# Mixer of a two-layer block: differential scores as three single-speed passes, sparse branch's side work and weight halves in other steps, another order where stages meet

## The chip, the cores and the metric

The kernel runs on one core of a Trainium2 chip. TensorE (PE) does the matrix products and transposes, VectorE (DVE) and ScalarE (ACT) the elementwise work and the copies out of PSUM, GpSimd (POOL) very little here, and SyncE (SP) issues most DMAs. Every engine has its own instruction stream and waits on semaphores of the others. The metric is the device time of one execution in microseconds; the times below are medians of runs of the same program.

## The reference, cut to what matters

```python
def second_block(x, ...):                      # after first_block, a hybrid layer
    for l in range(DEPTH_2):                   # 2 layers; x is 512 x 1024, fp32
        ...
        h = _rmsnorm(x, norm_g[l, 0]) * (1.0 + sc0) + sh0
        x = x + 0.5 * g0 * _swiglu(h, ffn_w_gate[l, 0], ffn_w_up[l, 0], ffn_w_down[l, 0])
        h = _rmsnorm(x, norm_g[l, 1]) * (1.0 + sc1) + sh1
        x = x + g1 * _token_mix(h, w_in[l], w_out[l], ...)
        h = _rmsnorm(x, norm_g[l, 2]) * (1.0 + sc2) + sh2
        x = x + 0.5 * g2 * _swiglu(h, ffn_w_gate[l, 1], ffn_w_up[l, 1], ffn_w_down[l, 1])
    return _rmsnorm(x, final_g)

def _token_mix(h, w_in, w_out, ...):
    z = h @ w_in
    (gu, gv, dq, dk, dv, nq, ...) = jnp.split(z, pts, axis=-1)
    y_a = _gmlp_sgu(gu, gv, ...)               # spatial gating, 4 groups of 64
    y_b = _diff_attention(dq, dk, dv, ...)     # "differential branch", 4 heads x 2 maps of 32
    y_c = _nsa(nq, ...)                        # "sparse branch", 8 heads of 64
    return jnp.concatenate([y_a, y_b, y_c], axis=-1) @ w_out

# in _diff_attention, for a block of 128 queries
        s = jnp.einsum('bhmqd,bhmkd->bhmqk', qi, k).astype(jnp.float32) * scale
        p = _masked_softmax(s, t[:, None] >= pos[None, :])
        a = p[:, :, 0] - lam * p[:, :, 1]
```

## The kernel before

The instruction streams of all engines are written out by hand; there is no scheduler. Each branch of a stage is a generator with numbered steps, one generator for each engine, and the stage's functions call next() on them between pieces of dense work. An engine runs its stream strictly in order, so what a step waits for holds back all that is written behind it.

**Dense products.** Activations and weights are kept as sums of two fp32r tensors, a high and a low one, and `three` (L545 to 548) forms each product with three matmuls: low activation by high weight (L546), high by high (L547), high by low (L548). fp32r is the form that TensorE streams in one pass; plain fp32 operands take two passes of it, which the trace records as two matmuls. A unit of weights, 128 partitions by 2048 columns, arrives as `raw`; ACT copies it into `w_hi` (L508) and DVE subtracts into `w_lo` (L514), in halves of 1024 columns. act_w and dve_w stand for these, and their last argument chooses a half.

**The order of stages.** After the first block come two layers, each of a gated feed-forward stage, the mixer and a second feed-forward stage. In the mixer, pe_mixer (L2782), act_mixer (L2895) and dve_mixer (L2987) run the differential branch (pe_da L2168, 22 steps) and the sparse branch (pe_nsa L2523, act_nsa L2736, dve_nsa L2654, 36 steps) between the dense products: input projections for the first part, and then the rows of the output projection, units o1_0, o1_1, o2_0, o2_1. PE is given one step of a branch after every few dense triples.

**Differential scores.** Queries and keys after rotation are `dq` and `dk`, fp32, four pieces of 128x512 (p = 0, 1 for dq, 2, 3 for dk), the last operation of each being an addition on DVE (L2159). In each of steps 0 to 15, PE multiplies one block of 128 queries by (b+1)*128 keys for two maps m (L2179). The contraction is only 32 long: the two maps use different groups of 32 rows of the array and different PSUM banks. Widths 512, 128, 384 and 256 take turns, four of each in a layer.

**Sparse branch.** Step s computes the scores of item s on PE (L2542) into two PSUM banks (N_SC). These banks come free when DVE has run `smallest` (L2664) on them, which finds the row minimum; ACT then takes the exponential, DVE runs `norm` (L2673, L2678), PE transposes, DVE or ACT copies back (L2646, L2644), and PE multiplies by the values (L2569). In dve_nsa the order inside a step is: smallest(s), copy, norm(s-1), and then the "side chains": the compressed-key scores (cm L2476, cx L2479 and L2481, cn), the gating branch's statistics g1, g3 (L2722, L2724), g5, gm, g7, g8, and the splits of finished pieces of the activation into high and low.

**Weight halves in the mixer.** Those of the output projection are prepared between steps. Before the change, ACT does the halves of o1_0 after steps 12 and 17, and DVE after 13 and 19; o1_1 follows on ACT after 20 and 22, o2_0 after 26 and 28. PE begins o1_0 two steps after item 16 and takes next(nsa) after every second activation row.

**Where the mixer meets the next stage.** pe_tail ends the mixer with unit o2_1; the second feed-forward stage begins in pe_first (L1903) with the units g and u, each for the first half of the sequence (H0, 256 columns) and then the second (H1). act_to_h (L1923) and dve_to_h (L1948) form its input from the residual update `xup` (L794), the statistics of the norm, and the modulation, which gives `h_hi` (L736) and `h_lo` (L745), one of eight pieces at a time.

## Time and profile before

| | us |
|---|---|
| median of the runs | 2634.02 (2633.14 to 2635.98, 3 runs) |
| profiled execution, its own time | 2635.69 |
| its span | 2634.3 |
| mean granted TensorE clock | 0.997 |

The span is the time from the first to the last instruction of the profiled execution; the 1.4 us around it belong to the launch. A timeline has one row for each instruction, or for a run of equal ones (x4), with its start in microseconds from the beginning of the span, its duration, and in square brackets the time that the engine idled before it and what released it. Matmuls are pipelined: a row's duration reaches past the start of the next one, so what a matmul costs is the distance from its start to the next start. The letter m below is a map, "step" is a numbered step of one of the branches, and "layer 1" lies 1011.1 us behind layer 0 with the same waits, so that one layer is enough to read.

### The profile page before, as it was taken

What the parts mean: (1) busy time and instruction counts of PE and PEld (TensorE: products, weight loads), DVE (VectorE), ACT (ScalarE), POOL (GpSimd) and SP (SyncE); (2) the same over time, 40 slices, a digit from 0 to 9 for tenths busy, and PEclk for the clock granted to TensorE, in tenths of its full rate; (3) what the DMA queues carried; (4) which work ended last, traced back from release to release, by engine and by line L of the source; (5) the groups of instructions that cost most, each with busy time, mean ns of one, the idle gap of its engine ahead of it and who ended that gap; (6) DMA issues with size and microseconds to landing.
All of it is one profiled execution on the core that took longest, in us unless ns stands there. A gap on an engine that the chain in (4) does not pass through costs nothing.

```text
span 2634.3 us, 33757 instructions
## 1 busy us (share of the span) xinstructions
PE 2602.2 (99%) x13925; PEld 2150.1 (82%) x13925; DVE 1558.8 (59%) x2769; ACT 1036.7 (39%) x1795; POOL 15.0 (1%) x43
## 2 busy tenths in 40 slices
PE   8999999999999999999999999999999999999999
PEld 5788888898888897767888889888888776888888
DVE  7766554458666366777766637653346687633334
ACT  4652343444222245665322225222234665422223
POOL 1000000000000000000000000000000000000000
PEclk9999999999999999999999999999999999999999
DMA  8255433225555234312655424532233501222222
GB/s 261 80 176 172 130 119 112 80 81 193 206 186 182 89 111 116 112 33 68 213 199 191 161 84 156 206 130 96 96 96 107 149 27 49 95 98 96 96 92 68
DMA packets 298241, 330.13 MB, mean 125 GB/s; under 512 B 13411, under 2 KB 248679, under 8 KB 298089
## 3 DMA queue, kind: packets, MB, share of 16 engines
q1 hardware_dynamic: 297716, 327.44, 38.2%
q8 instruction: 110, 1.80, 0.3%
q10 hardware_dynamic: 372, 0.55, 0.1%
q14 instruction: 43, 0.34, 0.0%
HBM read 319.56 MB, written 2.10 MB: 122 GB/s over the span
## 4 chain that ended last, share of the span: by engine, by line
PE 95%; DVE 4%; ACT 1%; DMA 0%; SPq 0%; issue 0%; DVEq 0%
PE bank L546 27%; PE bank L548 27%; PE bank L547 27%; PE bank L600 2%; PE bank L2542 2%; PE bank L2569 1%; PE bank L2179 1%; PE bank L574 1%; PE bank L575 1%; PE bank L576 1%; DMA mw<-in_w_mod 0%; PE bank L2354 0%; PE bank L903 0%; DVE w_lo L514 0%; DVE E L2678 0%; PE bank L590 0%
## 5 line engine op out<-in xcount | busy, mean ns | idle before, releaser
L546 PE MATMUL bank<-h_lo,w_hi 128*128 128x512 f32 (+1 forms) x2496 | 935.7, 375 | 2.3 <-DVE h_lo L745 1.2
L548 PE MATMUL bank<-h_hi,w_lo 128*128 128x512 f32 (+1 forms) x2496 | 918.5, 368 | 0.0
L547 PE MATMUL bank<-h_hi,w_hi 128*128 128x512 f32 (+1 forms) x2496 | 917.3, 368 | 0.0
L514 DVE TENSOR_TENSOR w_lo<-raw,w_hi 128x1024 fp32r<-128x1024 f32 (+1 forms) x420 | 489.1, 1200 | 373.5 <-ACT w_hi L508 373.3
L508 ACT ACTIVATE w_hi<-raw 128x1024 fp32r<-128x1024 f32 (+1 forms) x420 | 420.1, 1036 | 349.7 <-PE bank L548 335.4
L546 PEld LDWEIGHTS bank<-h_lo,w_hi 128*128 128x128 f32 x2496 | 471.0, 189 | 85.8 <-issue 4.9
L547 PEld LDWEIGHTS bank<-h_hi,w_hi 128*128 128x128 f32 x2496 | 471.4, 189 | 78.5 <-issue 3.9
L548 PEld LDWEIGHTS bank<-h_hi,w_lo 128*128 128x128 f32 x2496 | 470.3, 188 | 78.5
L546 PE MATMUL bank<-a_lo,w_hi 128*128 128x512 f32 (+1 forms) x1056 | 388.2, 368 | 4.4 <-DVE w_lo L514 4.4
L548 PE MATMUL bank<-a_hi,w_lo 128*128 128x512 f32 (+1 forms) x1056 | 384.8, 364 | 0.0
L547 PE MATMUL bank<-a_hi,w_hi 128*128 128x512 f32 (+1 forms) x1056 | 384.3, 364 | 0.0
L546 PEld LDWEIGHTS bank<-a_lo,w_hi 128*128 128x128 f32 x1056 | 199.5, 189 | 35.7 <-DVE w_lo L514 4.9
L548 PEld LDWEIGHTS bank<-a_hi,w_lo 128*128 128x128 f32 x1056 | 199.4, 189 | 31.4
L547 PEld LDWEIGHTS bank<-a_hi,w_hi 128*128 128x128 f32 x1056 | 199.6, 189 | 30.6
L767 ACT ACTIVATE a_hi<-tmp 128x512 fp32r<-128x512 f32 x104 | 65.5, 632 | 388.7 <-DVE tmp L2075 370.1
L794 DVE SCALAR_TENSOR_TENSOR x<-bank,small,x 128x512 f32<-128x512 f32 (+1 forms) x152 | 99.2, 663 | 182.0 <-PE bank L548 181.7
L2024 ACT ACTIVATE tmp<-bank 128x512 f32<-128x512 f32 x88 | 52.1, 596 | 292.8 <-PE bank L548 292.8
L2075 DVE TENSOR_TENSOR tmp<-tmp,bank 128x512 f32<-128x512 f32 x88 | 60.2, 684 | 124.8 <-PE bank L548 124.8
L771 DVE TENSOR_TENSOR a_lo<-tmp,a_hi 128x512 fp32r<-128x512 f32 x104 | 71.9, 692 | 68.6 <-ACT a_hi L767 68.4
L652 DVE SCALAR_TENSOR_TENSOR nacc<-swf,small,nacc 128x512 f32<-128x512 f32 x105 | 78.8, 751 | 3.2
L652 DVE SCALAR_TENSOR_TENSOR tmp<-swf,small,tmp 128x512 f32<-128x512 f32 x105 | 78.8, 751 | 3.2
L600 PEld LDWEIGHTS bank<-res,E 128*128 128x128 f32 x428 | 47.4, 142 | 27.0 <-issue 17.3
(347 smaller groups left out, 2283.7 us busy)
## 6 DMA issues: line engine op xcount, KB each, us to landing
swf<-in_w_ada SPq DMA_DIRECT2D x60, 1024.0 KB, 7.5
raw<-in_ffn_w_gate SPq DMA_DIRECT2D x44, 1024.0 KB, 5.2
raw<-in_ffn_w_up SPq DMA_DIRECT2D x44, 1024.0 KB, 5.2
raw<-in_w_in SPq DMA_DIRECT2D x40, 1024.0 KB, 5.0
raw<-in_ffn_w_down SPq DMA_DIRECT2D x32, 1024.0 KB, 5.3
raw<-in_w_in SPq DMA_DIRECT2D x32, 512.0 KB, 5.2
raw<-in_ffn_w_down SPq DMA_DIRECT2D x16, 768.0 KB, 4.4
mw<-in_w_mod SPq DMA_DIRECT2D x8, 1024.0 KB, 12.0
```

The source lines that it names most:

```text
L508: nc.scalar.activation(o, r, ACT.Copy).then_inc(*w_hi.up((i, h)))
L514: nc.vector.tensor_tensor(o, r, half(w_his[place_of[i]], i, h)[0].bitcast(F32), ALU.subtract).then_inc(*w_lo.up((i, h)))
L546: nc.tensor.matmul(o, w1, al, start=start, stop=False)
L547: nc.tensor.matmul(o, w1, ah, start=False, stop=False)
L548: return nc.tensor.matmul(o, w2, ah, start=False, stop=stop)
L600: return nc.tensor.transpose(o, i, ident[0:n, 0:n])
L652: nc.vector.scalar_tensor_tensor(acc, v[:, a, :], cv[:, k:k + 1], acc, ALU.mult, ALU.add).then_inc(*dve.up(("acc", st, j, k)))
L767: nc.scalar.activation(a_hi[:, c, :], src, ACT.Copy).then_inc(*act.up(("ah",) + key))
L771: nc.vector.tensor_tensor(a_lo[:, c, :], src, a_hi[:, c, :].bitcast(F32), ALU.subtract).then_inc(*dve.up(("a",) + key))
L794: nc.vector.scalar_tensor_tensor(x[:, c, COLS[hv]], ps.of(key)[:, COLS[hv]], gain[:, c:c + 1], x[:, c, COLS[hv]], ALU.mult, ALU.add).then_ ...
L2075: nc.vector.tensor_tensor(t, t, ps.of(("u", st, f))[:, :], ALU.mult).then_inc(*dve.up(("mul", st, f), lets=("u", st, f)))
L2542: nc.tensor.matmul(t[par][:, 0:w], nq[r, c * 512 + b * 128:c * 512 + b * 128 + 128], (ks, kw)[br][r, k0:k0 + w], start=True, stop=True).th ...
```

## The change

It has five parts.

1. **Differential scores.** The rotated queries and keys become high and low fp32r pairs, d_hi and d_lo. For each of the four pieces ACT makes a copy (act_da_high) and DVE a subtraction (dve_da_low). The scores of a step are then six fp32r matmuls in place of two fp32 ones (which the trace records as four): for each of low by high, high by low, high by high, both maps.
2. **Side chains of the sparse branch** are spread over more steps: cm in step 1 and cx in step 2 (before both in step 1), cn in step 4, g1 in step 9 and g3 in step 10 (before both in 9), gm in 12 at the latest, the second g7, g8 and split one to two steps later, the last subtraction of a finished output piece (OC_LOW) one step later, the transposes around steps 5 to 8 one step later.
3. **Weight halves in other steps.** o1_0: ACT after steps 12 and 14, DVE after 13 and 16. o1_1: ACT as before, DVE after 20 and 21 in its own count of pairs of steps, as shown in the diff. o2_0: ACT after 24 and 26, DVE correspondingly one pair earlier, and the first half of o2_1 before the end of the branch.
4. **Output rows between the last steps.** The dense work of o2_0 is written out, and steps 33, 34 and 35 of the sparse branch stand between its triples, not all ahead of it.
5. **Meeting order** after a mixer. The first half of u's weights is split in the tail, the norm's sums are taken from within g (at piece 4) to within u (at piece 3), u's banks are taken only when u begins, and the residual updates of the second half of the sequence stand after the modulation of the first, apart from one of them.

Cut to its core (name changes and the further shifts by one step are left out):

```diff
@@ sb tensors
-    dq = sb("dq", 1024, at=at_a + 16384 + 4096)
-    dk = sb("dk", 1024, at=at_a + 8192)
+    d_hi = [sb("dq_hi", 1024, F32R, at=at_a + 16384 + 4096), sb("dk_hi", 1024, F32R, at=at_a + 8192)]
+    d_lo = [sb(n, 1024, F32R, at=phase0 + 56256 + 4096 * i) for i, n in enumerate(("dq_lo", "dk_lo"))]
@@ act_tail, and the same with dve_w in dve_tail
+        if st[0] == "m":
+            act_w(first_of(nxt)[1], 0, 0)
@@ pe_first
-                    elif before(st) is not None and name == us[0][0] and j == 4:
+                    elif before(st) is not None and (name, j) == ((us[1][0], 3) if late else (us[0][0], 4)):
                         pe_sums(st, 1)
@@ act_to_h
+        if b4[0] == "m":
+            second = {3: [lambda: act_w(first[1], 0)], 6: second[1], 7: second[3] + second[5]}
+        else:
+            second[2] = [lambda: act_w(first[1], 0, 0)]
+            second[4] = [lambda: act_w(first[1], 0)]
@@ dve_to_h
+        elif b4[0] == "m":
+            second = dve_second(st, b4, gain)
+            dve_modulate(st, 0, mu, add, {5: second[0] + second[1]})
+            dve_w(first_of(st)[1], 0)
+            for i in range(2, 6):
+                second[i][0]()
@@ new
+    def act_da_high(l, p):
+        act.wait_ge(dve, ("rx", l, p))
+        nc.scalar.activation(da_part(d_hi, p), pair(p)[1][:, :], ACT.Copy).then_inc(*act.up(("rh", l, p)))
+
+    def dve_da_low(l, p):
+        dve.wait_ge(act, ("rh", l, p))
+        nc.vector.tensor_tensor(da_part(d_lo, p), pair(p)[1][:, :], da_part(d_hi, p).bitcast(F32), ALU.subtract).then_inc(
+            *dve.up(("rd", l, p)))
@@ pe_da
-                for m in range(2):
-                    t = bank(("ds", l, s, m), M_SC)
-                    pe.wait_ge(dve, ("rd", l, 3))
-                    r = slice((par * 2 + m) * 32, (par * 2 + m) * 32 + 32)
-                    nc.tensor.matmul(t[:, 0:w], dq[r, c * 512 + b * 128:c * 512 + b * 128 + 128],
-                                     dk[r, c * 512:c * 512 + w], start=True, stop=True).then_inc(*pe.up(("ds", l, s, m)))
+                for i, (dq, dk) in enumerate(((d_lo[0], d_hi[1]), (d_hi[0], d_lo[1]), (d_hi[0], d_hi[1]))):
+                    for m, r in enumerate(rows):
+                        mm = nc.tensor.matmul(t[m][:, 0:w], dq[r, q], dk[r, k], start=i == 0, stop=i == 2)
@@ dve_cm, dve_nsa
             if s == 1:
                 dve_cm(l, 1)
+            if s == 2:
+                dve_cx(l, 1)
@@ dve_nsa
             if s == 9:
                 dve.wait_ge(act, ("gl", l, 1))
                 nc.vector.tensor_reduce(m16, v3, AX, ALU.add).then_inc(*dve.up(("g1", l)))
-                dve.wait_ge(dve, PREV)
+            if s == 10:
+                dve.wait_ge(dve, ("g1", l))
                 nc.vector.scalar_tensor_tensor(v3, mb, -1.0 / 64, v3, ALU.mult, ALU.add).then_inc(*dve.up(("g3", l)))
@@ act_mixer
-                if m and s == 0:
-                    act_w(("gu", l), 1, 0)
+                if m and s in (0, 2):
+                    act_w(("gu", l), 1, s // 2)
...
-            if s == 17:
-                act_w(("gu", l))
             if s in (20, 22):
                 act_w(("o1", l, 0), 1, s // 22)
-            if s in (26, 28):
-                act_w(("o1", l, 1), 1, s // 28)
+            if s in (24, 26):
+                act_w(("o1", l, 1), 1, s // 26)
+            if s == 28:
+                act_w(("o2", l, 0), 1, 0)
@@ dve_mixer
         for c in range(NK):
-            for _ in range(2):
-                next(nsa)
-            if c == 1:
+            next(nsa)
+            if c == 0:
                 dve_w(("gu", l))
+            next(nsa)
             if c in (2, 3):
                 dve_w(("o1", l, 0), 1, c - 2)
-            if c in (5, 6):
-                dve_w(("o1", l, 1), 1, c - 5)
+            if c in (4, 5):
+                dve_w(("o1", l, 1), 1, c - 4)
+            if c == 6:
+                dve_w(("o2", l, 0), 1, 0)
@@ pe_mixer
-        for _ in nsa:
-            pass
+        next(nsa)
         u = unit(("o2", l, 0))
+        for j, k in enumerate(O2_ROWS):
+            pe.wait_ge(dve, ("a", ("m", l), k))
+            for c in range(4):
...
+                m = three(fills[c][:, :], w1, w2, a_lo[:, k, :], a_hi[:, k, :], j == 0, j == 3)
...
+                if (j, c) in ((0, 1), (1, 0), (1, 3)):
+                    next(nsa)
```

(The name in act_w and dve_w is the unit that runs while the next one is prepared: act_w(("gu", l), 1, 0) makes the first half of o1_0, act_w(("o1", l, 0), 1, ...) those of o1_1, act_w(("o1", l, 1), 1, ...) those of o2_0.)

How the change moves the instructions is seen at three places. The first is DVE in steps 1 and 2 of the sparse branch. `gmb<-gmb,hsum` ends step 1's small work, E_6_172 is the compressed-key score tile (cm, cx), E_4_170 and E_5_171 are the score tiles that `smallest` reads. Before:

```order
L2380 TENSOR_TENSOR gmb<-gmb,hsum 64x256
L2476 TENSOR_TENSOR E_6_172<-bank,res 128x512
L2479 TENSOR_REDUCE small<-E_6_172 128x16
L2481 TENSOR_TENSOR E_6_172<-E_6_172,small 128x512
L2664 ISA E_4_170,small<-bank,res 128x128
L2664 ISA small 128x1
L2664 ISA E_5_171,small<-bank,res 128x128
```

With the change:

```order
L2413 TENSOR_TENSOR gmb<-gmb,hsum 64x256
L2508 TENSOR_TENSOR E_6_172<-bank,res 128x512
L2699 ISA E_4_170,small<-bank,res 128x128
L2699 ISA small 128x1
L2699 ISA E_5_171,small<-bank,res 128x128
L2699 ISA small 128x1
L2708 RECIPROCAL small<-small 128x2
L2713 TENSOR_SCALAR E_2_168<-E_2_168,small,gates 128x512
L2713 TENSOR_SCALAR E_3_169<-E_3_169,small,gates 128x512
L2514 TENSOR_REDUCE small<-E_6_172 128x16
L2516 TENSOR_TENSOR E_6_172<-E_6_172,small 128x512
```

The reduction and the subtraction now stand behind the next step's `smallest` and norm instead of ahead of them.

The second place is DVE around the second low half of o1_0 (w_lo_59). Before, it stands behind step 19:

```order
L2646 COPY tmp_64<-bank 128x512
L2673 RECIPROCAL small<-small 128x2
L2678 TENSOR_SCALAR E_4_170<-E_4_170,small,gates 128x128
L2678 TENSOR_SCALAR E_5_171<-E_5_171,small,gates 128x128
L514 TENSOR_TENSOR w_lo_59<-raw_54,w_hi_57 128x1024
L794 SCALAR_TENSOR_TENSOR x<-bank,small,x 128x512
L2664 ISA E_0_166,small<-bank,res 128x384
```

With the change it stands behind step 16:

```order
L2681 COPY tmp_173<-bank 128x384
L2708 RECIPROCAL small<-small 128x2
L2713 TENSOR_SCALAR ex_179<-ex_179,small,gates 128x256
L2713 TENSOR_SCALAR ex_180<-ex_180,small,gates 128x256
L514 TENSOR_TENSOR w_lo_59<-raw_54,w_hi_57 128x1024
L2699 ISA E_2_168,small<-bank,res 128x512
L2699 ISA small 128x1
```

It moved up by three steps of the branch and one residual update.

The third place is PE at the end of the sparse branch, between the last transposes (L600) and the last products with the values (L2569 before, L2604 after; `vsw`). Before:

```order
L600 MATMUL bank<-res,ex_179 128x128 x2
L600 MATMUL bank<-res,ex_180 128x128 x2
L2569 MATMUL bank<-ps_175,vsw 64x128
L2569 MATMUL bank<-ps_176,vsw 64x128
L2569 MATMUL bank<-ps_175,vsw 64x128
L2569 MATMUL bank<-ps_176,vsw 64x128
```

With the change:

```order
L600 MATMUL bank<-res,ex_179 128x128 x2
L600 MATMUL bank<-res,ex_180 128x128 x2
L546 MATMUL bank<-a_lo,w_hi_57 128x512
L547 MATMUL bank<-a_hi,w_hi_57 128x512
L548 MATMUL bank<-a_hi,w_lo_59 128x512
L546 MATMUL bank<-a_lo,w_hi_57 128x512
L547 MATMUL bank<-a_hi,w_hi_57 128x512
L548 MATMUL bank<-a_hi,w_lo_59 128x512
L546 MATMUL bank<-a_lo,w_hi_57 128x512
L547 MATMUL bank<-a_hi,w_hi_57 128x512
L548 MATMUL bank<-a_hi,w_lo_59 128x512
L2604 MATMUL bank<-ps_175,vsw 64x128
```

Three triples of o2_0 now stand between the transposes and the products that use what is copied back from them.

## Rows read from the trace of the kernel before

**Rows 1.** Page, part 1: busy time of each engine and share of the span.

```profile
PE 2602.2 (99%) x13925; PEld 2150.1 (82%) x13925; DVE 1558.8 (59%) x2769; ACT 1036.7 (39%) x1795; POOL 15.0 (1%) x43
```

**Rows 2.** Waits of PE: released line, releaser, total us, times, longest.

```profile
PE bank L546 <- DVE w_lo L514: 5.4, 4, 2.2
...
PE bank L2542 <- DVE small L2664: 1.4, 4, 0.5
PE bank L546 <- DVE h_lo L745: 1.2, 4, 0.3
PE bank L2604 <- DVE gvv L2730: 0.7, 2, 0.4
...
PE bank L600 <- DVE ps L2646: 0.6, 2, 0.3
```

**Rows 3.** Timeline of PE: fp32 products on 32 rows, two full-array ones.

```profile
1016.43 1.13 PE L2179 MATMUL bank<-dk,dq 32*128 32x512 f32 x4
1017.49 0.50 PE L546 MATMUL bank<-h_lo,w_hi 128*128 128x512 f32 x1
...
1024.43 0.49 PE L2179 MATMUL bank<-dk,dq 32*128 32x128 f32 x4
1024.85 0.50 PE L546 MATMUL bank<-h_lo,w_hi 128*128 128x512 f32 x1
...
72.40 1.02 PE L1112 MATMUL bank<-uc,wrg 128*128 128x512 f32 x2
73.26 1.02 PE L1114 MATMUL bank<-uc,wig 128*128 128x512 f32 x2
```

**Rows 4.** Timeline of PE: starts of dense fp32r triples of 512 and 256 columns.

```profile
1236.11 0.39 PE L546 MATMUL bank<-a_lo,w_hi 128*128 128x512 f32 x1
...
1236.79 0.28 PE L546 MATMUL bank<-a_lo,w_hi 128*128 128x256 f32 x1
...
1237.15 0.28 PE L546 MATMUL bank<-a_lo,w_hi 128*128 128x256 f32 x1
```

**Rows 5.** Timeline of DVE: the last addition of the rotated keys.

```profile
1010.76 0.69 DVE L2159 TENSOR_TENSOR dk<-swap,tmp 128x512 f32<-128x512 f32 x1
```

**Rows 6.** Timeline, DVE and then PE: sparse steps 1 to 3.

```profile
1105.49 0.68 DVE L2476 TENSOR_TENSOR E<-bank,res 128x512 f32<-128x512 f32 x1
...
1106.92 0.69 DVE L2481 TENSOR_TENSOR E<-E,small 128x512 f32<-128x512 f32 x1
1107.53 0.28 DVE L2664 CUSTOM_DVE_ANT_0 E<-bank,res 128x128 f32<-128x128 f32 x1
...
1108.18 0.49 PE L2542 MATMUL bank<-kw,nq 64*128 64x128 f32 x4 [1.32 <-DVE small L2673]
```

**Rows 7.** DVE, PE; windows: length; busy PE, PEld, DVE, ACT, POOL, clock, DMA share, GB/s.

```profile
1173.25 1.22 DVE L514 TENSOR_TENSOR w_lo<-raw,w_hi 128x1024 fp32r<-128x1024 f32 x1
...
1174.53 0.50 PE L546 MATMUL bank<-a_lo,w_hi 128*128 128x512 f32 x1 [2.19 <-DVE w_lo L514]
...
1175.80:1179.20 3.40, 3.40 (x12) 1.73 (x11) 1.11 (x5) 0.00 (x0) 0.00 (x0) 0.50 0.88 298
1174.53:1184.95 10.42, 10.42 (x64) 6.50 (x65) 4.66 (x14) 4.52 (x11) 0.00 (x0) 0.84 0.32 102
1204.89:1213.72 8.83, 8.83 (x67) 5.73 (x66) 6.88 (x19) 5.12 (x12) 0.00 (x0) 1.00 0.00 0
```

**Rows 8.** Timeline, PE and then DVE: the meeting after the mixer of layer 0.

```profile
1251.63 0.39 PE L546 MATMUL bank<-h_lo,w_hi 128*128 128x256 f32 x1 [0.15 <-DVE h_lo L745]
1252.95 0.39 PE L546 MATMUL bank<-h_lo,w_hi 128*128 128x256 f32 x1 [0.35 <-DVE h_lo L745]
1257.86 0.39 PE L546 MATMUL bank<-h_lo,w_hi 128*128 128x256 f32 x1 [0.52 <-DVE w_lo L514]
...
1259.65 0.48 DVE L745 SCALAR_TENSOR_TENSOR h_lo<-tmp,small,h_hi 128x256 fp32r<-128x256 f32 x1
...
1260.44 0.48 DVE L745 SCALAR_TENSOR_TENSOR h_lo<-tmp,small,h_hi 128x256 fp32r<-128x256 f32 x1
```

More of the change, by code:

```diff
@@ L335, in carve, with here @@
         place = [start]
-        def here(name, cols):
-            t = sb(name, cols, at=place[0])
+        def here(name, cols, dt=F32):
+            t = sb(name, cols, dt, at=place[0])
             place[0] += (cols * 4 + 63) // 64 * 64
@@ L1903, in pe_first @@
     def pe_first(st, units_, ring):
-        us = [(name, unit(name), [(key, bank(key, ring)) for key in keys]) for name, keys in units_]
+        us, fills_of = [(name, unit(name), keys) for name, keys in units_], {}
+        late = before(st) is not None and before(st)[0] == "m"
+        if not late:
+            fills_of = {name: [(key, bank(key, ring)) for key in keys] for name, _, keys in us}
         for hv in range(2):
-            for name, u, fills in us:
+            for name, u, keys in us:
                 def hook(j):
@@ L1916, in hook @@
                         pe_norm(st, 1)
-                    elif before(st) is not None and name == us[0][0] and j == 4:
+                    elif before(st) is not None and (name, j) == ((us[1][0], 3) if late else (us[0][0], 4)):
                         pe_sums(st, 1)
+                if name not in fills_of:
+                    fills_of[name] = [(key, bank(key, ring)) for key in keys]
+                fills = fills_of[name]
                 dense(name, fills if hv else [(None, t) for _, t in fills], u, 0, H, NK,
@@ L2123, in rope_where @@
         every = slice(0, 128)
-        if p < 2:
-            d = [(every, dq[:, p * 512:p * 512 + 512])]
-        elif p < 4:
-            d = [(every, dk[:, (p - 2) * 512:(p - 2) * 512 + 512])]
+        if p < 4:
+            d = [(every, pair(p)[1][:, :])]
         elif p < 8:
@@ L2737, in act_nsa @@
         for s in range(36):
+            m16 = stl[0][:, 0:16]
             if s % 2 == 0:
                 nsa_copy(act, l, s - 3)
+            if s == 12:
+                act.wait_ge(dve, ("g5", l))
+                nc.scalar.activation(m16, m16, use(ACT.Ln), scale=1.0 / 64, bias=eps_c).then_inc(*act.up(("gn", l)))
+                act.wait_ge(act, PREV)
+                nc.scalar.activation(m16, m16, use(ACT.Exp), scale=-0.5).then_inc(*act.up(("g6", l)))
             if s < 32:
@@ L2910, in act_mixer @@
         act_w(("dv", l))
-        for tb in range(4):
-            act_dv(l, tb)
+        act_dv(l, 0)
+        act_dv(l, 1)
+        act_da_high(l, 2)
+        act_dv(l, 2)
+        act_da_high(l, 3)
+        act_dv(l, 3)
         da = act_da(l)
@@ L3010, in dve_mixer @@
         dve_rope(l, 1)
+        dve_da_low(l, 0)
+        dve_da_low(l, 1)
         dve_w(("dv", l))
```

91 lines of the change are left out of this document (53 added, 38 removed).

## The prediction

> **What bounds the kernel now.** I read the busy times first. PE is busy for 2602.2 of 2634.3 us [rows 1], so whatever is gained must come out of the few microseconds in which PE waits, or out of the matmuls themselves. DVE (59%) and ACT (39%) have room on average, and only their order can hurt. The second view is the list of what PE waits for [rows 2]. Nearly all of it in the mixer is DVE's: the low half of a weight (5.4 us in 4 waits), the release of score banks, the gating branch's `gvv`. The third is PE's timeline around each of these waits, and there DVE's rows just ahead of it. The waits come in pairs, one for each layer, so I cost one layer and double it.
>
> **Scores of the differential branch.** Before, a step of width 512 takes 1017.49 - 1016.43 = 1.06 us from its start to the next operation's, and one of width 128 takes 1024.85 - 1024.43 = 0.42 [rows 3]. The line through both is 0.20 + 0.00167 us for each column, which puts widths 256 and 384 at 0.63 and 0.85. Does the pair of maps run side by side or one after the other? One full-array fp32 product of 512 columns, in its two passes (x2), takes 73.26 - 72.40 = 0.86 us [rows 3]. Two maps in 1.06 us are 0.20 + 0.86, so the pair costs one product: they run together on their different rows. The 0.20 does not grow with the width.
>
> After, a step is three passes of such a pair. A dense fp32r pass takes (1236.79 - 1236.11) / 3 = 0.227 us for 512 columns and (1237.15 - 1236.79) / 3 = 0.12 for 256 [rows 4], so about 0.173 for 384. For 128 no such pass is in these rows: 0.06 is the floor (half of 256), 0.12 the ceiling. I take 0.12, since changing the stationary operand costs the same however few columns stream. That makes 0.20 + 0.68 = 0.88, 0.72, 0.56 and 0.56 us, against 1.06, 0.85, 0.63 and 0.42: -0.18, -0.13, -0.07 and +0.14, together -0.24 us. Each width comes four times a layer: **-1.0 us**. With the floor for width 128 it would be -1.7.
>
> Are the loads of the later passes hidden? The second pass of today's step has no load of its own in the sum: width 128 comes out at 0.42 with 0.20 fixed, which leaves 0.11 for each pass and nothing beside it [rows 3]. The Trainium skill speaks against that for the new passes ("TensorE: Matmul & The Clock Gate", Part 3, The mechanism): a weight load overlaps a running matmul only if the two use different row groups, and here each pass reloads the rows of the pass before. By the rows the sum for the scores is -1.0 a layer, by the rule it would be +1.4; the rows of today's two passes don't agree with the rule, so it is rival 2 with a small chance.
>
> The pairs' preparation adds four ACT copies and four DVE subtractions of 128x512 a layer, some 0.7 us each by the addition of the same size [rows 5]. The last rotated key is written at 1010.76 + 0.69 = 1011.45, the first score starts at 1016.43 [rows 3, 5]. 5.0 us cover the last subtraction and what ACT puts in front of it (some 2.7 us by the same price), so I cost it at nothing. If the cover were gone, each further us would be one on the path.
>
> **Side chains.** The scores of sparse step 3 wait 1.32 us for score banks [rows 6]. DVE runs the two operations of cx (the second ends at 1107.53, the first began after cm's start at 1105.49) ahead of `smallest`, which begins at 1107.53. Without cx it begins after cm alone, 0.7 us after 1105.49, so 1.3 us earlier, and the wait is gone: **-1.3**. What is late next is `smallest` of step 3, behind the displaced cx. From step 3 to step 4 PE has 0.42 of scores, 1.44 of four triples of 256 columns [rows 4] and, as an estimate, 1.0 of transposes, 2.9 in all; DVE has `smallest` 0.4, norm 1.1, cx 1.3, 2.8 in all. It is on the edge, and I leave 0 to 0.3 us for it in the range. The same mechanism stands behind one of the two L2542 waits in a layer that are released by `smallest` (L2664: 1.4 us in 4, [rows 2]; the longest, 0.5, is behind g1 and g3, which the change puts into two steps): **-0.5**; the other one, 0.2 at step 1, stays. The `gvv` wait, 0.4, goes with gm a step earlier: **-0.4**.
>
> **Weight halves.** At 1174.53 o1_0's third block had waited 2.19 us for a low half that DVE began at 1173.25, 1.22 us long [rows 7]. The subtraction now stands three steps and one residual update earlier. A step is some 4 us of PE's time, and the wait is about 2.2, so it goes with room: **-2.2**. What follows that wait counts as well: from 1175.80 to 1179.20 the granted clock is 0.50, that is 1.2 GHz in place of 2.4, and PE had just stood still for 2.19 us. The stretch 1174.53 to 1184.95 holds 64 matmuls in 10.42 us, the like stretch 1204.89 to 1213.72 67 in 8.83 at clock 1.00 [rows 7]: 1.6 us. I expect the clock to stay up if PE does not stop: **-1.6**. Against it stands that the DMA share in those 3.4 us is 0.88, so that something other than the idle time could be the cause; that is a rival.
>
> **Output rows between the last steps.** The wait of 0.3 for the last copy back (L2646 to `ps`) [rows 2] is covered by three triples, 2.0 us at 0.68 [rows 4]: **-0.3**. These steps' banks come free later by that much, which nobody needs.
>
> **Meeting.** Before, PE waits 0.15, 0.35 and 0.52 us here [rows 8]. The third, for u's low weights, goes, because half of them is split in the tail. DVE makes one piece of `h_lo` every 1260.44 - 1259.65 = 0.79 us [rows 8], and PE uses it up in two triples of 256 columns, 0.72 us [rows 4], so small waits stay. The second half's pieces now come behind four residual updates and one low half of 1.22 us that follow the modulation, about when PE is there. I take 0.4 of the 1.0 us as left: **-0.6**, with bounds -1.0 (all three gone) and +0.5 (the second half late by one low half, 1.2, less what the third gives).
>
> **Exposed loads.** A matmul after a wait has its weight load in the open: 0.50 us against 0.39 for the same operation [rows 4, 7], 0.1. Five waits go: **-0.5**.
>
> **The sum** for a layer is -1.0 - 1.3 - 0.5 - 0.4 - 2.2 - 1.6 - 0.3 - 0.6 - 0.5 = -8.4 us, for both -16.8. The profiled execution was 2635.69 us with a span of 2634.3; it would be 2618.9 with 2617.5. It lies 1.7 above the median of 2634.02, so against the median the forecast is **2617.2 us**, with a range of its own of 2613 to 2621.5 (narrow passes at their floor -1.4, the meeting -0.8 or +2.2, the displaced cx +0.6, 1.5 for unseen shifts).
>
> **The rivals.**
> 1. *The clock drops all the same, and waits return.* Everything on DVE moves earlier, but DVE's work in the mixer is not less, it has four subtractions more. If the half clock belongs to the DMA burst, +3.2; if `smallest` waits return at half their size behind cx and the splits, +1.8 to +3. Together some +6.3: 2623.5 us. For it: the DMA share in the half-clock stretch. Against it: no other wait of the mixer's is followed by such a stretch.
> 2. *The load of each pass in the open.* The second and third pass of the three wider widths take 0.1 more each: 24 steps by 0.2, +4.8; a pass of 128 columns has its load in the 0.12 already: 2622.0 us. Against it is the width-128 step above. This is what the skill's rule would give.
> 3. *The pairs don't run together in fp32r.* The rows show pairs only for plain fp32. Six passes in a row are 0.20 + 6 x 0.227 = 1.56, 1.24, 0.92, 0.92 us: +0.50, +0.39, +0.29, +0.50, that is +1.7 for four widths, +13.4 in place of -1.9 for the kernel: 2632.5 us, no change that could be measured.
> 4. *The same, and a load in the open at every change of rows*: five more of 0.1 us in 32 steps, +16: 2648.5 us, **slower**. It decides from where a step costs more than about 0.5 us above the present one, on the average of the widths (0.5 x 32 = 16, which eats up the other gains). For it: a change between full-array and 32-row work costs 0.20 today. Against it: the pair of today starts together.
> 5. *The weight half does not come earlier.* The order permits it, but its raw weights may arrive late: the 2.2 and 1.6 us of both layers stay, 2617.2 + 7.6 = 2624.8 us. Against it: the first half of the same unit is already being used when PE waits.
>
> **How the numbers follow.** Forecast 0.60, rival 1 0.18, rival 2 0.08, rival 3 0.04, rival 4 0.05, rival 5 0.05. A measurement of this kernel can tell 0.2%, 5.3 us, from no change. Below 2628.7 lie the forecast and rivals 1, 2 and 5, 0.91, of which I take off 0.04 for waits that I have not seen: faster 0.87, within 0.2% 0.08, slower 0.05. From 2612 to 2627 lie the forecast's own range but for a tenth, rivals 1, 2 and 5 and most of what is between them: about 0.8.
>
> **What would show it.** In the profile after: a score step of the differential branch of 0.88 us at width 512 and 0.56 at 128 (1.56: rival 3; 1.06 and 0.7: rival 2); no L546 wait for `w_lo` above 0.3 us and a clock of 1.00 where o1_0's third block runs; no L2542 wait above 0.3 in sparse step 3 and step 10; waits of some 0.4 in all at the meeting. The prediction is wrong if PE's list of waits has a new entry of a microsecond or more in the mixer, or if PE's busy time rises.

## The result and the profile after

| | before | changed | ratio, 95% interval |
|---|---|---|---|
| median of the runs, us | 2633.58 (2631.75 to 2635.98, 4 runs) | 2620.74 (2619.85 to 2622.49, 4 runs) | 0.9947 (0.9936 to 0.9959) |
| profiled execution, us | 2635.69 | 2622.49 | |
| its span, us | 2634.3 | 2621.2 | |

The change makes the kernel 14.0 us faster by the ratio (10.8 to 16.9). The forecast was a gain of 16.8 us and a time of 2617.2 us, with a range of 2612 to 2627. The busy times and the list of PE's waits answer to [rows 1] and [rows 2]:

```profile
PE 2593.9 (99%) x13989; PEld 2153.6 (82%) x13989; DVE 1562.8 (60%) x2777; ACT 1041.1 (40%) x1803; POOL 15.0 (1%) x43
```

```profile
PE bank L2577 <- DVE small L2699: 2.9, 6, 0.6
...
PE bank L2211 <- DVE small L2296: 1.3, 2, 0.6
PE bank L709 <- DVE nacc L703: 1.0, 2, 0.5
```

L2577 is the line of the sparse scores (L2542 before), L2211 that of the differential ones (L2179), L2699 `smallest` (L2664), L2681 the copy back (L2646). The 5.4 us of waits for `w_lo` are gone, and so are the 1.3 us at step 3 and `gvv`. What is waited for score banks of the sparse branch behind `smallest` has grown: six waits of 2.9 us where four made 1.4 (plus 2.6 behind the norm). Two entries are new, 1.3 us for score banks of the differential branch (L2211) and 1.0 us for the norm's sums (nacc). The prediction had said that a new entry of a microsecond or more in the mixer would show it wrong; this sign came, although the time is inside the range. PE's busy time, its other sign, fell from 2602.2 to 2593.9 us. Of the 1.3 us at L2211 little is a loss: before, a pause of 0.53 us stood inside the same step, between its two maps, where no wait is listed.

Both kernels issue the same dense matmuls in the same order, so the start of the n-th one can be compared between the two traces. I call these the dense starts. Their differences, taken across one place after another, divide the gain. Layer 1, in us:

| place | forecast (with its load, 0.1 each) | measured |
|---|---|---|
| differential scores, 16 steps | -1.0 | -1.15 |
| banks at sparse step 3 | -1.4 | -1.37 |
| banks behind g1, g3 | -0.6 | -0.60 |
| `gvv` | -0.5 | -0.43 |
| low half of o1_0 | -2.3 | -2.47 |
| half clock behind it | -1.6 | -1.56 |
| banks at sparse step 23 | 0 | +0.60 |
| last steps of the sparse branch, the banks at step 31 included | -0.4 | -0.33 |
| norm's first sums | 0 | +0.78 |
| rest of the meeting | -0.6 | -1.04 |
| sum | -8.4 | -7.57 |

Layer 0 gives -7.64. Both give -15.2; the spans differ by only 13.1, since the changed kernel's profiled execution had lost 2.06 us before the first mixer, in code that the change doesn't touch: 0.4 at the start and 1.67 at 612 to 620 us, where the granted clock stayed low for longer (below).

The score steps, answering to [rows 3]:

```profile
1018.49 0.49 PE L2211 MATMUL bank<-dk_hi,dq_lo 32*128 32x512 f32 x2
1018.82 0.40 PE L2211 MATMUL bank<-dk_lo,dq_hi 32*128 32x512 f32 x2
1019.05 0.40 PE L2211 MATMUL bank<-dk_hi,dq_hi 32*128 32x512 f32 x2
1019.38 0.50 PE L546 MATMUL bank<-h_lo,w_hi 128*128 128x512 f32 x1
...
1026.16 0.33 PE L2211 MATMUL bank<-dk_hi,dq_lo 32*128 32x128 f32 x2
1026.32 0.27 PE L2211 MATMUL bank<-dk_lo,dq_hi 32*128 32x128 f32 x2
1026.43 0.27 PE L2211 MATMUL bank<-dk_hi,dq_hi 32*128 32x128 f32 x2
1026.63 0.50 PE L546 MATMUL bank<-h_lo,w_hi 128*128 128x512 f32 x1
```

Width 512 takes 1019.38 - 1018.49 = 0.89 us (1.06 before, 0.88 forecast), width 128 takes 0.48 (0.42 before, 0.56 forecast). The two maps of a pass start together (x2). The third pass follows the second at 0.23 and 0.11 us, with no load in the open, while the second follows the first at 0.33 and 0.16. At widths 384 and 256 the steps take 0.72 and 0.55.

DVE at sparse steps 1 and 2, answering to [rows 6]:

```profile
1106.42 0.68 DVE L2508 TENSOR_TENSOR E<-bank,res 128x512 f32<-128x512 f32 x1
1107.02 0.27 DVE L2699 CUSTOM_DVE_ANT_0 E<-bank,res 128x128 f32<-128x128 f32 x1
...
1108.54 0.68 DVE L2514 TENSOR_REDUCE small<-E 128x16 f32<-128x512 f32 x1
1109.26 0.69 DVE L2516 TENSOR_TENSOR E<-E,small 128x512 f32<-128x512 f32 x1
```

`smallest` now starts 0.6 us after cm began; before, 2.04 us after it. PE has no wait there.

The stretch from the start of o1_0's third block, answering to the windows of [rows 7] (columns as there):

```profile
1170.59:1180.20 9.61, 9.61 (x70) 6.39 (x69) 7.00 (x22) 5.92 (x14) 0.00 (x0) 1.00 0.00 0
```

The clock is 1.00 all through, and there is no wait. At the meeting none of the three waits of [rows 8] is in the list any more. But over the second half of the sequence PE now runs at DVE's pace, every second triple 0.79 us behind the last one where it was 0.72 before:

```profile
1258.83 0.36 PE L546 MATMUL bank<-h_lo,w_hi 128*128 128x256 f32 x1
...
1259.62 0.36 PE L546 MATMUL bank<-h_lo,w_hi 128*128 128x256 f32 x1
```

One place did not go as forecast: PE waits for score banks at sparse step 23, which the `smallest` of step 22 releases. The rows show this wait, and then what DVE does meanwhile:

```profile
1184.10 0.70 PE L2577 MATMUL bank<-kw,nq 64*128 64x256 f32 x4 [0.63 <-DVE small L2699]
...
1180.79 0.68 DVE L2752 TENSOR_TENSOR a_lo<-bank,a_hi 128x512 fp32r<-128x512 f32 x1
1181.39 1.22 DVE L514 TENSOR_TENSOR w_lo<-raw,w_hi 128x1024 fp32r<-128x1024 f32 x1
1182.52 0.75 DVE L794 SCALAR_TENSOR_TENSOR x<-bank,small,x 128x512 f32<-128x512 f32 x1
1183.18 0.41 DVE L2699 CUSTOM_DVE_ANT_0 E<-bank,res 128x256 f32<-128x256 f32 x1
```

Three operations, 2.4 us, stand in DVE's queue ahead of `smallest`: the subtraction of a finished output piece, moved there by OC_LOW, a weight half and a residual update. The last two stood there before the change as well, and the subtraction one step earlier, where DVE had been idle:

```profile
1181.98 0.69 DVE L2715 TENSOR_TENSOR a_lo<-bank,a_hi 128x512 fp32r<-128x512 f32 x1 [1.44 <-ACT a_hi L2766]
...
1186.31 1.22 DVE L514 TENSOR_TENSOR w_lo<-raw,w_hi 128x1024 fp32r<-128x1024 f32 x1
1187.45 0.74 DVE L794 SCALAR_TENSOR_TENSOR x<-bank,small,x 128x512 f32<-128x512 f32 x1
1188.11 0.41 DVE L2664 CUSTOM_DVE_ANT_0 E<-bank,res 128x256 f32<-128x256 f32 x1
```

So this half of o1_1 is not one of those that the change moved on DVE; the diff has its line unchanged. The same three kinds of operation meet again eight steps later, where PE waits 0.63 us at step 31. And at the norm's sums:

```profile
1239.33 0.70 PE L709 MATMUL bank<-nacc,res 128*128 128x256 f32 x2 [0.52 <-DVE nacc L703]
...
1222.69 0.43 DVE L2681 COPY ps<-bank 128x256 f32<-128x256 f32 x1 [2.09 <-PE bank L600]
1226.64 0.69 DVE L2752 TENSOR_TENSOR a_lo<-bank,a_hi 128x512 fp32r<-128x512 f32 x1 [3.52 <-ACT a_hi L2811]
1227.59 3.50 DVE L514 TENSOR_TENSOR w_lo<-raw,w_hi 128x1024 fp32r<-128x1024 f32 x3 [0.26 <-ACT w_hi L508]
```

DVE stands idle for 2.09 and 3.52 us, and then has three low halves in a row, behind which the updates and the sums are late.

### The profile page after: what moved, and what is told of

Its sections match the earlier page's. It is cut to its first block, busy times and chain, and to the rows that moved or that the text cites. A ratio compares the mean times of both kernels' runs of the same rounds, so it can differ in the third digit from the quotient of the medians.

```text
span 2621.2 us, 33927 instructions
## 1 busy us (share of the span) xinstructions
PE 2593.9 (99%) x13989; PEld 2153.6 (82%) x13989; DVE 1562.8 (60%) x2777; ACT 1041.1 (40%) x1803; POOL 15.0 (1%) x43
## 4 chain that ended last, share of the span: by engine, by line
PE 95%; DVE 3%; ACT 1%; DMA 0%; SPq 0%; issue 0%; DVEq 0%
PE bank L546 27%; PE bank L548 27%; PE bank L547 27%; PE bank L600 3%; PE bank L2577 2%; PE bank L2604 2%; PE bank L2211 1%; PE bank L574 1%; PE bank L575 1%; PE bank L576 1%; DVE w_lo L514 1%; DMA mw<-in_w_mod 0%; PE bank L907 0%; PE bank L2387 0%; DVE x L794 0%; PE bank L590 0%
## 5 line engine op out<-in xcount | busy, mean ns | idle before, releaser
L600 PE MATMUL bank<-res,E 128*128 128x128 f32 x428 | 67.8, 283 | 0.6 <-DVE tmp L2681 0.6
```

What stands on the lines that cost most here:

```text
L600: return nc.tensor.transpose(o, i, ident[0:n, 0:n])
```

## Experiments

**One part alone: the scores (e1_split).** The kernel before with the preparation and the scores of the change, as in the diff ahead.

> The kernel before with one part of the change: the differential scores as three fp32r passes of a pair of maps, with their four copies and four subtractions a layer. Theory: the new passes run in pairs and their weight loads are hidden, whatever stands around them. A step should take 0.89, 0.72, 0.55 and 0.48 us at widths 512, 384, 256 and 128, as in the profile of the changed kernel, instead of 1.06, 0.85, 0.63 and 0.42: -0.31 for each set of four widths, eight sets, -2.5 us in all, about 2631.1. Rival: the preparation (eight operations more on ACT and DVE) delays what follows, so that part of it is lost, and the time stays within 1 us of before.

Median 2633.44 us against 2635.42 in the same session, ratio 0.9993 (0.9984 to 1.0003): a gain of 1.8 us that is not clear of noise. The dense starts show it more sharply: -1.11 us across the differential branch in layer 0 and -1.13 in layer 1, with no loss behind it, 2.2 us in all. The rest of the expected 2.5 went to PE's wait for score banks in the last step (0.65 us; before it was 0.53 and stood between the two maps of that step).

**One part alone: the weight half (e2_half).** The kernel before with

```diff
-                if m and s == 0:
-                    act_w(("gu", l), 1, 0)
+                if m and s in (0, 2):
+                    act_w(("gu", l), 1, s // 2)
...
-            if s == 17:
-                act_w(("gu", l))
...
-            for _ in range(2):
-                next(nsa)
-            if c == 1:
+            next(nsa)
+            if c == 0:
                 dve_w(("gu", l))
+            next(nsa)
```

> The kernel before with one part of the change: the second weight half of o1_0 on ACT after step 14 (17 before) and on DVE after step 16 (19 before). Theory: PE's wait of 2.19 us in each layer goes and the half-clock stretch behind it goes too, since it follows from PE's standing still: 2 x (2.47 + 1.56) = -8.1 us, about 2625.5, clock 1.00 in the 10 us after the start of o1_0's third block. Rival: the clock falls because of the DMA burst there (share 0.88): only -4.9 us, about 2628.7, and a stretch at clock 0.50 remains.

2627.63 against 2635.42, ratio 0.9973 (0.9963 to 0.9983), 7.1 us. The dense starts move by -4.04 us at o1_0's third block in layer 0 and by -4.03 in layer 1, as expected. The stretch with the DMA burst is there without the fall of the clock:

```profile
1167.40:1170.80 3.40, 3.40 (x23) 2.64 (x22) 3.14 (x9) 1.80 (x6) 0.00 (x0) 1.00 0.96 291
```

These are the columns of the windows in [rows 7]: the clock is 1.00 at a DMA share of 0.96, where it was 0.50 at 0.88 over a window of the same length. The burst alone is not what lowers it.

**The part undone (e3_late).** The changed kernel with the reverse of that edit.

> The changed kernel with the same part undone: the second weight half of o1_0 again after steps 17 (ACT) and 19 (DVE). Theory: the wait for the low half is back in both layers with about 2.2 us or somewhat more (PE arrives 4 us earlier than before, but DVE is also earlier), and with it the stretch of some 3.4 us at half clock, +8 us against the changed kernel, about 2628.8. Rival: the wait comes back without the half clock, +5 us, about 2625.7; that would make the clock's fall a coincidence with a DMA burst.

2632.72 us, ratio 0.9986 (0.9977 to 0.9996) where the changed kernel had 0.9947: 10.3 us slower than it. The dense starts give +6.0 in layer 0 and +4.7 in layer 1. This is more than the expected 8 us, and the wait gives one part of it:

```profile
1174.00 0.79 PE L546 MATMUL bank<-a_lo,w_hi 128*128 128x512 f32 x1 [2.92 <-DVE w_lo L514]
```

PE comes earlier than before and waits 2.92 us, not 2.19. The clock gives the other part: in layer 0 it is at 0.50 for 6.8 us, from 1173.4 to 1180.2, and in layer 1 for 3.4 us, as in both layers before the change. The ten runs of this kernel lie between 2626.5 and 2633.9 us, the changed kernel's four between 2619.9 and 2622.5.

What the clock does behind this wait was not the same each time, though. In e1_split, which has the wait of before in both layers, layer 1 shows the half clock and layer 0 doesn't:

```profile
1173.44 0.50 PE L546 MATMUL bank<-a_lo,w_hi 128*128 128x512 f32 x1 [2.19 <-DVE w_lo L514]
...
1171.50:1173.50 2.00, 0.06 (x1) 0.06 (x1) 1.96 (x6) 0.38 (x1) 0.00 (x0) 1.00 0.00 0
1173.50:1177.00 3.50, 3.50 (x19) 2.41 (x20) 1.57 (x6) 0.00 (x0) 0.00 (x0) 1.00 0.71 195
```

So in five of the six profiled passages with this wait the clock fell (two layers of three kernels), and in none of the eighteen without it (two layers of nine kernels). At this place the fall comes only behind the wait, but not behind each.

**The order of the maps (e4_maps).** The changed kernel with

```diff
-                for i, (dq, dk) in enumerate(((d_lo[0], d_hi[1]), (d_hi[0], d_lo[1]), (d_hi[0], d_hi[1]))):
-                    for m, r in enumerate(rows):
+                for m, r in enumerate(rows):
+                    for i, (dq, dk) in enumerate(((d_lo[0], d_hi[1]), (d_hi[0], d_lo[1]), (d_hi[0], d_hi[1]))):
```

> The changed kernel with the six score matmuls of a step in another order: the three passes of the first map, then the three of the second, on other rows of the array. Theory: two maps run together only when their matmuls follow each other directly, so six passes stand in a row: 0.20 + 6 x 0.227 = 1.56 us at width 512 and 1.24, 0.92 and 0.7 to 0.9 at 384, 256 and 128, against 0.89, 0.72, 0.55 and 0.48, together +1.8 to +2.0 for four widths and +14 to +16 us in all, about 2635. Rival: TensorE overlaps matmuls on different rows whatever their order, within its queue: no change, 2620.7; or an overlap at the seam only, one pass in six, about +11.

2621.77 us, ratio 0.9949 (0.9934 to 0.9964), the same as the changed kernel's 0.9947. The theory that adjacency makes the pair is wrong, the first rival holds. The timeline shows the pairs as before although each map's three passes stand together in the program:

```profile
1017.71 0.50 PE L2211 MATMUL bank<-dk_hi,dq_lo 32*128 32x512 f32 x2
1018.04 0.40 PE L2211 MATMUL bank<-dk_lo,dq_hi 32*128 32x512 f32 x2
1018.27 0.41 PE L2211 MATMUL bank<-dk_hi,dq_hi 32*128 32x512 f32 x2
1018.61 0.50 PE L546 MATMUL bank<-h_lo,w_hi 128*128 128x512 f32 x1
```

It takes 0.90 us from the first start to the next operation, 0.89 in the other order. The two starts of a pair are 0.010 us apart here and 0.003 in the changed kernel, so the order in the program leaves a trace, but a small one: 0.1 us a layer by the dense starts.

**The new waits for banks (e5_low).** The changed kernel with

```diff
-    OC_STEP, OC_LOW = (12, 20, 28, 35), (13, 21, 29, 35)
+    OC_STEP, OC_LOW = (12, 20, 28, 35), (13, 22, 30, 35)
```

> The changed kernel with one more shift: DVE's subtraction of a finished output piece (a_lo) in steps 22 and 30 instead of 21 and 29, so behind those steps' smallest and norm. Theory: the two new waits of PE for score banks in a layer (0.63 us each) come from a queue on DVE of a_lo 0.6, w_lo 1.14 and a residual update 0.66 ahead of smallest; without a_lo the banks come free 0.6 us earlier, and both waits go: -0.63 and its exposed load 0.1, twice a layer, -2.9 us in all, about 2617.8. Rival: the wait is set by the low half and the residual update, or a_lo only delays the next step's copy: -1 us or less.

2619.86 us, ratio 0.9945 (0.9928 to 0.9962), not to be told from the changed kernel's by time. The dense starts show half of the theory: -0.61 at step 23 and then +0.13, and only -0.05 around step 31. There the wait for banks is gone too, but this one has grown from 0.32 us:

```profile
1212.97 1.23 PE L600 MATMUL bank<-res,E 128*128 128x128 f32 x6 [0.75 <-DVE tmp L2681]
```

The subtraction, one step later, stands ahead of the copy for which PE waits next. The queue is the cause at both places, but at the second the shift only hands the wait on. Two other runs show that the earlier half of o1_0 has no part in these waits: e2_half, which has it but leaves the subtraction in its old step, has no wait for score banks at steps 23 and 31, and e3_late, which has the subtraction in its new step but not the earlier half, waits 0.64 and 0.63 us there.

**The wait for the sums (e6_tail).** The changed kernel with the second half of o2_1 after step 33; DVE's part is shown, ACT's is the same:

```diff
+        next(nsa)
+        next(nsa)
+        dve_w(("o2", l, 0))
         for _ in nsa:
             pass
-        dve_w(("o2", l, 0))
         dve_w(("o2", l, 1))
```

> The changed kernel with the second weight half of o2_1 made before the last two steps of the sparse branch, on ACT and DVE, instead of behind it. Theory: the new wait at the norm's sums (nacc, 0.52 us and a load in the open, 0.78 in all, a layer) is DVE's backlog of three low halves (3.5 us) behind the branch, in front of which it stood idle for 3.5 us; one of them put into that gap brings everything behind it 1.1 us earlier: -0.78 a layer, -1.6 us in all, about 2619.1. Rival: what is late is not DVE's backlog but the last of PE's own results that it updates with, or the gain is lost again at the next wait of the meeting: no change.

2619.13 us, ratio 0.9941 (0.9926 to 0.9956). The dense starts move by -0.78 at this place and nowhere else; the wait for nacc is no longer among PE's. The low half now runs in the gap:

```profile
1219.80 1.23 DVE L514 TENSOR_TENSOR w_lo<-raw,w_hi 128x1024 fp32r<-128x1024 f32 x1 [1.16 <-ACT w_hi L508]
...
1225.61 2.36 DVE L514 TENSOR_TENSOR w_lo<-raw,w_hi 128x1024 fp32r<-128x1024 f32 x2 [0.26 <-ACT w_hi L508]
```

**The interleaving undone (e7_nointer)**, with all remaining steps ahead of one dense call for o2_0, as before the change.

> The changed kernel with one part undone: steps 33 to 35 of the sparse branch all ahead of the dense rows of o2_0. Theory: the interleaving saved about 1.0 us a layer around the last steps (waits for copies back of 0.3 to 0.4 and their exposed loads), and gave 0.78 of it back at the norm's sums, where PE now comes earlier than DVE; undone, the stretch up to o2_0's rows is 1.0 longer and the wait at the sums gone: +0.2 a layer, +0.4 in all, 2621.1. Rival: the wait at the sums has another cause and stays: +2 us, 2622.7.

2621.43 us, ratio 0.9948 (0.9933 to 0.9963). By the dense starts, +0.97 up to o2_0's rows and -0.78 at the norm's sums, +0.19 for the layer: what the interleaving gains, it hands to DVE's backlog almost whole. PE's wait for the last copy is back, and the products with the values behind it take longer than in the changed kernel, whose row is the last one:

```profile
1219.33 0.66 PE L600 MATMUL bank<-res,ex 128*128 128x128 f32 x4 [0.30 <-DVE ps L2681]
1219.92 1.29 PE L2604 MATMUL bank<-ps,vsw 128*64 128x128 f32 x16
...
1224.87 1.09 PE L2604 MATMUL bank<-ps,vsw 128*64 128x128 f32 x16
```

The starts inside these rows show why. In e7_nointer the ninth of the sixteen products starts 0.25 us after the eighth, and in the row of 24 products ahead of them (1.86 us against 1.53) the thirteenth starts 0.38 us after the twelfth; in the changed kernel both distances are 0.10. These pauses stand in no list of waits, since each row reaches past the next start.

**The meeting order undone (e8_meet)**: pe_first, act_to_h, dve_to_h and the two tails as before.

> The changed kernel with one part undone: the old order where the mixer meets the next stage. Theory: the new order takes 1.04 us out of each layer behind the norm's first sums and has no part in the wait at those sums: undone, +1.0 a layer, +2.1 in all, 2622.8, with PE's waits for h_lo and u's low half (0.15, 0.35, 0.52 before) back. Rival: the early arrival of PE alone took these waits away or turned them into others, and the order is worth little: within 0.5 us of the changed kernel.

2623.97 us, ratio 0.9958 (0.9943 to 0.9973). By the dense starts +1.04 for the layer, all behind the first sums, and the three waits of [rows 8] come back in their old sizes:

```profile
1246.78 0.39 PE L546 MATMUL bank<-h_lo,w_hi 128*128 128x256 f32 x1 [0.16 <-DVE h_lo L745]
1248.11 0.39 PE L546 MATMUL bank<-h_lo,w_hi 128*128 128x256 f32 x1 [0.35 <-DVE h_lo L745]
1253.02 0.39 PE L546 MATMUL bank<-h_lo,w_hi 128*128 128x256 f32 x1 [0.52 <-DVE w_lo L514]
```

**cx back in step 1 (e10_cx).** The changed kernel with dve_cx called directly behind dve_cm.

> The changed kernel with one part undone: the two operations of cx again directly behind cm, in step 1, ahead of the smallest of step 2. Theory: they are 1.33 us in DVE's queue ahead of what PE waits for at the scores of step 3, and nothing else of the side chains matters there: the wait of 1.3 us is back with its exposed load, +1.4 a layer, +2.8 in all, 2623.5. Rival: the other shifts of the side chains and the shorter differential branch have given DVE enough lead that less than half of it returns: +1 us or less.

2624.54 us, ratio 0.9957 (0.9942 to 0.9973). By the dense starts +1.37, all at this place:

```profile
1109.22 0.49 PE L2577 MATMUL bank<-kw,nq 64*128 64x128 f32 x4 [1.32 <-DVE small L2708]
```

The wait is the old one to the hundredth.

**A version with the repairs (e9_best)**: e6_tail's edit, OC_LOW = (13, 22, 32, 35), and in the differential branch

```diff
         dve_rope(l, 8)
+        steps(1)
         dve_w(("kk", l), 2)
-        steps(1)
         dve_rope(l, 9)
```

> The changed kernel with three shifts on DVE. (1) The half of o2_1 before the last two steps of the sparse branch, as in e6_tail: -0.78 a layer. (2) a_lo of the second output piece in step 22, and that of the third in step 32, behind the last smallest, where in e5_low step 30 only turned PE's wait for score banks into one for the copy of step 31: -0.61 and -0.73 a layer. (3) In the differential branch the second low half of the unit that PE uses next (vv) one step later, so that it is not queued ahead of the smallest for which PE waits 0.65 us: -0.75 a layer. Theory: DVE's queue ahead of these four points is the whole cause of the four waits: -2.87 a layer, -5.7 in all, about 2615.0. Rival: the third shift makes PE wait for the low half itself, or the step-32 subtraction comes too late for o2's rows; each would give back what its shift brings: about 2616.5 to 2617.5.

2616.39 us (2615.97 to 2619.05, 5 runs) against 2634.93, ratio 0.9931 (0.9918 to 0.9943): 18.2 us faster than before, and the lowest of all kernels here. The intervals of this ratio and of the changed kernel's overlap, so the gain over the latter rests on the dense starts: -1.84 us in layer 1, of which -0.78 at the sums, -0.60 at step 23 (then +0.12) and -0.60 around step 31. The third shift brought nothing, +0.03. PE's wait of 0.65 for banks is gone, and two others stand in its place:

```profile
1076.49 0.52 PE L600 MATMUL bank<-res,E 128*128 128x128 f32 x3 [0.30 <-DVE E L2280]
1079.38 0.88 PE L2225 MATMUL bank<-tmp,dvn 128*64 128x128 f32 x12 [0.48 <-ACT tmp L2259]
```

The rival was right that something would give it back, but not in how: neither for a low half nor for o2's rows does PE wait. PE now waits once for DVE and, longer than before, once for ACT there; which of their operations would have to become shorter or move was not tried. By time the kernel stands at the rival's 2616.5 and not at the theory's 2615.0.

## Why the prediction held, point by point

**What bounds the kernel** was read rightly: each gain is a wait of PE that ended in DVE's queue, the half clock behind one of them, or time saved in the matmuls, and both layers gave the same within 0.1 us.

**Scores.** The pair of maps runs together in fp32r and the later loads are hidden. The steps of 0.89 and 0.48 us in the changed kernel and in e1_split rule out rivals 2, 3 and 4. The rule of the Trainium skill ("TensorE: Matmul & The Clock Gate", Part 3, The mechanism), by which a weight load overlaps a running matmul only if the two use different row groups, finds no support here: the third pass follows the second, on the same rows, at 0.23 us, as in dense triples. What makes three fp32r passes cheaper than one fp32 product is that an fp32 product is recorded as two passes of 0.43 us each [rows 3], not of 0.227 as an fp32r pass [rows 4]; "two passes" in the description of the dense products is a count of records, not a price. The mis-sized term was the step of width 128, 0.56 forecast and 0.48 measured: its passes are 0.11 apart and not 0.12, and the fixed part, 0.20 at width 512, is 0.15 here. So -0.31 came for four widths where -0.24 was forecast. Part of that went to the wait for banks in the last step, and -1.0 became -1.15, not -1.24. Costing the eight preparing operations at nothing was right: in e1_split nothing behind them moved.

**Side chains.** The three terms -1.4, -0.6 and -0.5 (loads included) measured -1.37, -0.60 and -0.43, and e10_cx brought the first back alone. The displaced cx cost nothing. The step that failed is here: of the side chains the prediction costed cx, g1 and g3, and gm, and put the later subtraction of a finished output piece (OC_LOW) at nothing without a reason. In its old step DVE was idle ahead of it; in the new one a weight half and a residual update stand behind it, all three ahead of one `smallest`. The prediction looked at what stood ahead of the operations that were moved and not at what they would now stand ahead of. It cost 0.6 twice in a layer, +2.4 in all. Rival 1 had this size as "waits return" (1.8 to 3 us). Its place, "behind cx and the splits", was half right: the subtraction is such a split, and cx had no part. Its other half, the clock, did not come.

**Weight halves.** -2.3 and -1.6 measured -2.47 and -1.56; e2_half brought 4.0 us in each layer alone, with no new wait. That a listed wait of 2.19 cost 2.47 holds for the other dense waits too: it is counted from the end of a row that reaches past the next start, so the load's 0.1 was too little to add.

**Last steps.** -0.4 was forecast for the one wait. The interleaving is worth -0.97 (e7_nointer). Of this 0.53 us are the pauses inside the rows of products, which the list of waits does not show and the prediction could not take from it; the two blocks of products are 0.33 and 0.20 us shorter in the changed kernel. That they are waits for the second half of a copy back is likely but not shown. Of the gain the second new wait for banks, +0.60, is to be taken. At the norm's sums +0.78 came: the prediction did not see that PE, once earlier, would find DVE's three low halves in its way. "These steps' banks come free later, which nobody needs" was right; what it left out is the engine that does not get faster with PE.

**Meeting.** -0.6 was forecast and -1.04 came (e8_meet brings +1.04 back). That "small waits stay" was right: DVE makes a piece every 0.79 us, PE would need 0.72, and over the second half of the sequence this costs 0.43 us, though no wait is listed. A further 0.34 is lost around 1248.4, where PE starts just as DVE ends a piece. Together that is more than the 0.4 that was taken as left. What was too small is the price of the three waits: by the starts on both sides they cost 0.41, 0.60 and 0.83 us, 1.8 in all, and not the listed 1.0. The two of them that were for h_lo did not come from the pace of 0.79 either. They stood in the first half of the sequence, where an update or a sum between the pieces had made it 1.2 to 1.3 us; the change takes most of these out.

**The clock.** That the half-clock stretch comes from PE's wait is supported by e2_half and e3_late. The DMA burst of rival 1 is ruled out as the cause by itself: e2_half has it at clock 1.00, and at another place (below) the clock stays at 0.50 with a DMA share of 0.00. That the stretch is certain to follow the wait, and that it is 3.4 us long, was too much: one passage of six had no fall, and one had 6.8 us.

**The sum**: -8.4 a layer forecast, -7.6 measured. The errors are +1.2 for banks, +0.78 for the sums, -0.57 for the interleaving, -0.44 for the meeting and -0.15 for the scores, and small ones. They partly cancel, so the sum came nearer than its terms by some luck. A few small readings of the prediction don't come out, and none moves the forecast: the second operation of cx ends at 1107.61 and not 1107.53, the upper bound of the meeting, 1.2 less 0.52, is +0.7 and not +0.5, the terms of the range reach down to 2613.5 and not 2613, and those of rival 1 make at most 6.2 and not 6.3.

## What to carry to other kernels

When an engine off the critical path does its work in a fixed order, cost a moved operation at both ends: what its old place frees, and what its new place queues up behind it, together with what already stands there. A microsecond that the bounding engine gains can be a microsecond of lead that the others lose; go on down the program with the new arrival time until a gap of theirs absorbs it. Take what a wait costs from the starts on both sides of it and not from the idle time in its row, and look inside rows of many equal operations, where pauses stand that no list of waits has. A helper's idle gap directly ahead of its backlog, as here 3.5 us ahead of three weight halves, is where to look first.

## What was not expected of the hardware

**Matmuls on different rows of the array pair up even when they don't follow each other in the program.** With three passes of one map written ahead of the three of the other, the second map's first pass, fourth in the program, started 0.01 us after the first map's and before its second pass, in all 32 steps, and the step took 0.90 us against 0.89. Within such a step PE does not start its matmuls in the order of the program, so that "strictly in order", as the kernel's description has it for every engine, does not hold here.

**Behind a wait of PE of about 2 us the granted clock often fell, but not always.** There is a second place of this kind, the meeting of the two blocks, which no kernel here changes. Each of the twelve profiled executions has a wait of 1.90 or 1.91 us there, and what followed was different. The changed kernel's execution, waits and then the windows behind them:

```profile
612.04 0.70 PE L917 MATMUL bank<-nacc,res 128*128 128x256 f32 x2 [1.90 <-DVE nacc L936]
...
614.00:616.00 2.00, 1.40 (x7) 1.10 (x7) 1.82 (x6) 1.20 (x3) 0.00 (x0) 0.50 0.00 0
616.00:618.00 2.00, 2.00 (x11) 2.00 (x11) 2.00 (x7) 1.23 (x3) 0.00 (x0) 0.50 0.00 0
```

The same place in e9_best:

```profile
610.83 0.70 PE L917 MATMUL bank<-nacc,res 128*128 128x256 f32 x2 [1.90 <-DVE nacc L936]
...
614.00:616.00 2.00, 1.88 (x14) 1.83 (x15) 2.00 (x7) 1.02 (x2) 0.00 (x0) 1.00 0.00 0
616.00:618.00 2.00, 2.00 (x18) 1.95 (x17) 2.00 (x7) 1.36 (x3) 0.00 (x0) 1.00 0.00 0
```

By such windows the clock stayed at 1.00 in four of the twelve; it was at 0.50 for about 3.4 us in three, and for about 6.8 us in five (the clock's shortfall in the windows, doubled). Between the profiled executions of the two kernels this is 1.67 us that have nothing to do with the change; the four runs of the changed kernel differ by 2.6 us. What decides between the three cases stays open.
